# Gated attention's first three norm sums taken as two rounded products each

## The reference, cut to what matters

```
def rms_norm_2(x, gain):
    x32 = x.astype(jnp.float32)
    y = x32 * lax.rsqrt(jnp.mean(x32 * x32, axis=-1, keepdims=True) + EPS)
    return (y * gain.astype(jnp.float32)).astype(x.dtype)
```

## Time and profile before

| what | us |
|---|---|
| median of 3 runs | 2284.31 |
| lowest and highest run | 2283.43, 2285.08 |
| the profiled execution, its own time | 2283.69 |
| its span, first to last instruction | 2281.9 |
| TensorE busy | 2270.4 |
| VectorE busy | 1677.5 |
| ScalarE busy | 1321.6 |

### The profile page before, as it was taken

The page is one execution under the profiler, slowest core; times in us unless marked ns, Lnnn a source line. Parts: engine busy times, 40 slices in busy tenths (PEclk is TensorE's granted clock), DMA queues, the critical chain, the costliest instruction groups (busy, mean ns, idle before and its releaser), DMA issues.

```text
span 2281.9 us, 36209 instructions
## 1 busy us (share of the span) xinstructions
PE 2270.4 (99%) x14199; PEld 1997.4 (88%) x14199; DVE 1677.5 (74%) x2130; ACT 1321.6 (58%) x1630; POOL 66.3 (3%) x104
## 2 busy tenths in 40 slices
PE   8999999999999999999999999999999999999999
PEld 7888888988888889889888888998888888889888
DVE  7876678787667666778776776688875677777773
ACT  7554567566456445675654654666654565467552
POOL 3200002000000000000000000000000000000000
PEclk9999999999999999999999999999999999999999
DMA  8655656565555555545655555534555565644653
GB/s 252 205 186 192 189 159 167 174 202 184 186 186 190 193 184 181 158 149 184 199 189 191 187 188 184 173 107 151 185 184 188 181 195 191 212 130 153 191 190 129
DMA packets 344946, 411.91 MB, mean 181 GB/s; under 512 B 7812, under 2 KB 291926, under 8 KB 344704
## 3 DMA queue, kind: packets, MB, share of 16 engines
q1 hardware_dynamic: 340432, 399.30, 54.0%
q0 software_dynamic: 4176, 10.95, 2.0%
q10 hardware_dynamic: 224, 0.07, 0.0%
HBM read 409.08 MB, written 1.21 MB: 180 GB/s over the span
## 4 chain that ended last, share of the span: by engine, by line
PE 97%; DVE 1%; DMA 1%; ACT 0%; issue 0%; SPq 0%; DVEq 0%; ACTq 0%
PE ps L605 54%; PE ps L608 27%; PE ps L633 2%; PE ps L634 1%; PE ps L635 1%; PE ps L650 1%; PE ps L652 1%; PE ps L651 1%; PE ps L902 1%; PE ps L979 1%; PE ps L980 1%; PE ps L981 1%; PE ps L931 1%; PE ps L915 1%; DMA raw<-in_w_mem_kv 0%; PE ps L1113 0%
## 5 line engine op out<-in xcount | busy, mean ns | idle before, releaser
L605 PE MATMUL ps<-h,whi 128*128 128x512 f32 x3552 | 1120.7, 396 | 0.1
L1983 DVE TENSOR_TENSOR wlo<-raw,whi 128x2048 fp32r<-128x2048 f32 x375 | 859.0, 2292 | 272.1 <-ACT whi L1340 270.9
L1340 ACT ACTIVATE whi<-raw 128x2048 fp32r<-128x2048 f32 x376 | 719.6, 1915 | 268.4 <-DMA raw<-in_ffn_w_down 157.2
L608 PEld LDWEIGHTS ps<-h,wlo 128*128 128x128 f32 x3552 | 666.3, 188 | 161.8
L608 PE MATMUL ps<-h,wlo 128*128 128x256 f32 x3552 | 702.6, 279 | 0.0
L605 PEld LDWEIGHTS ps<-h,whi 128*128 128x128 f32 x3552 | 539.1, 188 | 6.4 <-issue 5.7
L605 PE MATMUL ps<-act,whi 128*128 128x512 f32 x1408 | 444.7, 396 | 0.0
L1383 ACT ACTIVATE accT<-ps 128x512 f32<-128x512 f32 x227 | 135.4, 596 | 372.8 <-PE ps L608 372.2
L608 PEld LDWEIGHTS ps<-act,wlo 128*128 128x128 f32 x1408 | 264.7, 188 | 65.8
L608 PE MATMUL ps<-act,wlo 128*128 128x256 f32 x1408 | 278.4, 278 | 0.0
L1992 DVE TENSOR_TENSOR accT<-ps,accT 128x512 f32<-128x512 f32 x200 | 138.2, 691 | 166.3 <-ACT accT L1383 165.0
(11 more groups left out here) (407 smaller groups left out, 2329.2 us busy)
## 6 DMA issues: line engine op xcount, KB each, us to landing
raw<-in_ffn_w_gate SPq DMA_DIRECT2D x88, 1024.0 KB, 5.3
raw<-in_ffn_w_up SPq DMA_DIRECT2D x88, 1024.0 KB, 5.3
raw<-in_ffn_w_down SPq DMA_DIRECT2D x88, 1024.0 KB, 5.0
raw<-in_w_in SPq DMA_DIRECT2D x30, 1024.0 KB, 5.4
raw<-in_w_gate SPq DMA_DIRECT2D x24, 1024.0 KB, 5.4
raw<-in_w_in_a SPq DMA_DIRECT2D x13, 1024.0 KB, 5.2
raw<-in_w_branch SPq DMA_DIRECT2D x12, 1024.0 KB, 5.1
raw<-in_w_o SPq DMA_DIRECT2D x8, 1024.0 KB, 5.2
```

The lines of the kernel that those rows point to most:

```text
L605: mm(dst, whi[:, r, col:col + P], rhs, start=first, stop=False, skip_group_check=True)
L608: return mm(dst[:, 0:SEQ], wlo[:, r, col:col + P], rhs[:, 0:SEQ], start=False, stop=last, skip_group_check=True)
L1340: fn(whi[:, gr % RING, :], raw[:, gr % RING, :], ACT.Copy).then_inc(hi_done, 1)
L1983: v.tensor_tensor(wlo[:, gr % RING, :], raw[:, gr % RING, :], whi[:, gr % RING, :].bitcast(F32), ALU.subtract)\
```

## The change

The sums of the first three pairs in the stage `fox` become two products of rounded (fp32r) operands each, added in PSUM; the fourth pair's sum stays as it is.

- ScalarE's squares are written in the rounded format (`qn_r` or `sq_r[:, 6:8]`, the same memory as before). They are the high part, and no instruction is added on ScalarE.
- VectorE squares the same pair again in full float32 into a free part of `sq` (`tensor_tensor`, 128x512), waits for ScalarE's square, and subtracts the high part in place (`low_part`, 128x512), which leaves the low part. Both stand right behind the scaling of slots 0, 1 and 2, and `low_part` signals the new semaphore `qn_low`.
- TensorE waits for `qn_low` in place of `qn_sq` and runs `two_parts`: `blk_r` times the high part, `blk_r` times the low part, in the same place of the order as the product at L731.
- `blk_r`, a rounded copy of `blk` (128x128), is made once by VectorE in slot 0 of the stage `kv`, some 230 us earlier.
- `sq` gets a second view of type fp32r at the same place, and its allocation grows by 32 bytes, so that what lies behind it moves by that much.

The diff, cut to its core:

```diff
+            def two_parts(b, high, low):
+                fill(b)
+                mm(ps[:, b, :], blk_r[:, :], high, start=True, stop=False)
+                mm(ps[:, b, :], blk_r[:, :], low, start=False, stop=True).then_inc(filled[b], 1)
+
-            def qk_norm(src=qn, b=7):
+            def qk_norm(src=qn, b=7, low=None):
                 n.q += 1
+                if low is not None:
+                    n.low += 1
+                    pe.wait_ge(qn_low, n.low)
+                    two_parts(b, src[:, :, :].rearrange("p a n -> p (a n)"), low.rearrange("p a n -> p (a n)"))
+                    return
                 pe.wait_ge(qn_sq, n.q)
...
                             if s_ == 2:
                                 pe.wait_ge(summed, n.e + 2)
-                                qk_norm(qn, 3)
+                                qk_norm(qn_r, 3, low=sq_r[:, 2:4, :])
                             elif s_ in (3, 4):
-                                qk_norm(qn if s_ == 3 else sq[:, 6:8, :], 3)
+                                qk_norm(qn_r if s_ == 3 else sq[:, 6:8, :], 3, low=sq_r[:, 2:4, :] if s_ == 3 else None)
...
-                            hooks = {2: third, 3: lambda: qk_norm(sq[:, 6:8, :])}
+                            hooks = {2: third, 3: lambda: qk_norm(sq_r[:, 6:8, :], low=sq_r[:, 4:6, :])}
...
-                            qk_squares(fqm[:, :, :], (summed, n.e + 1), free=1)
+                            qk_squares(fqm[:, :, :], (summed, n.e + 1), qn_r, 1)
...
-                            qk_squares(fq[:, 0:2, :], (summed, n.e + 2), sq[:, 6:8, :], 1)
+                            qk_squares(fq[:, 0:2, :], (summed, n.e + 2), sq_r[:, 6:8, :], 1)
...
-                            qk_squares(fq[:, 2:4, :], (summed, n.e + 3), free=1)
+                            qk_squares(fq[:, 2:4, :], (summed, n.e + 3), qn_r, 1)
...
+            def low_part(low, full, high, squares):
+                dve.wait_ge(qn_sq, squares)
+                v.tensor_tensor(low, full, high.bitcast(F32), ALU.subtract).then_inc(qn_low, 1)
...
+                        if s == 0:
+                            v.tensor_copy(blk_r[:, :], blk)
...
                         v.tensor_tensor(dst, src, rstd2, ALU.mult).then_inc(summed, 1)
+                        if s < 3:
+                            k, high = (4, sq_r[:, 6:8, :]) if s == 1 else (2, qn_r[:, :, :])
+                            full = sq[:, k:k + 2, :]
+                            dve.wait_ge(summed, n.e + s + 1)
+                            link(v.tensor_tensor(full, dst, dst, ALU.mult))
+                            low_part(sq_r[:, k:k + 2, :], full, high, q0 + s + 1)
```

More of the change, by code:

```diff
@@ L92, in __init__ @@
         self.q = 0
+        self.low = 0
         self.post = 0
@@ L236, in mixed_transformer @@
         xT = sb("xT", [P, KT, SEQ])
-        sq = sb("sq", [P, KT, SEQ])
+        sq_base = (nc.sbuf_base + 31) // 32 * 32
+        sb("squares", [P, KT * SEQ + 8])
+        sq = nc.alloc_sbuf_tensor_at("sq", [P, KT, SEQ], F32, offset=sq_base)
+        sq_r = nc.alloc_sbuf_tensor_at("sq_r", [P, KT, SEQ], F32R, offset=sq_base)
         h = sb("h", [P, KT, 2 * SEQ], F32R)
@@ L259, in mixed_transformer @@
         qn = nc.alloc_sbuf_tensor_at("qn", [P, 2, SEQ], F32, offset=qn_base)
+        qn_r = nc.alloc_sbuf_tensor_at("qn_r", [P, 2, SEQ], F32R, offset=qn_base)
         hll = nc.alloc_sbuf_tensor_at("hll", [P, 2, TT, P], F32R, offset=qn_base)
@@ L283, in mixed_transformer @@
         junk = at("junk", 68 * K, [P, D_MODEL])
+        qm_r = at("qm_r", 64 * K, [P, DEPTH, 2, SEQ], F32R)
+        junk_r = at("junk_r", 68 * K, [P, D_MODEL], F32R)
         diag = at("diag", 72 * K, [P, 4, P])
@@ L289, in mixed_transformer @@
         onat = at("onat", 0, [P, TT, D_MODEL])
+        blk_r = at("blk_r", 87 * K + 512, [P, P], F32R)
         act = at("act", 0, [P, FT, 2 * SEQ], F32R)
@@ L368, in mixed_transformer @@
         qn_sq, qn_rs, qn_done = sem("qn_sq"), sem("qn_rs"), sem("qn_done")
+        qn_low, mk_low = sem("qn_low"), sem("mk_low")
         f_gate, lf_done = sem("f_gate"), sem("lf_done")
@@ L1408, in qk_norm, with qk_squares @@
                 qk_roots()
-            def qk_squares(src, ready, dst=qn, free=0):
+            def qk_squares(src, ready, dst=qn, free=0, full=None):
                 act_e.wait_ge(*ready)
@@ L1413, in qk_squares @@
                     act_e.wait_ge(qn_done, n.q - free)
+                if full is not None:
+                    fn(full, src, ACT.Square)
                 fn(dst[:, :, :], src, ACT.Square).then_inc(qn_sq, 1)
@@ L2806, in step @@
                         scaled(i)
+                    q0 = n.q
                     for s in range(7):
```

## The result

The changed kernel takes 2287.22 us (20 runs, 2286.85 to 2287.98) against 2283.77 us for the kernel before (20 runs, 2283.01 to 2285.08): a ratio of 1.0015, 95% interval 1.001 to 1.0021. It is 3.45 us slower where 1.2 us faster was forecast.

The account below looks back on a forecast made before the run. The prediction took TensorE, busy in 99% of the span, as the bound. Three sums saving 1.17 us, all else at nothing, took the profiled 2283.69 to 2282.5 us and the median from 2284.31 to 2283.1, range 2281.4 to 2285.1.

Parts of the forecast that it names:

- last sign of being wrong: Whole span: the prediction is wrong if what the stage `fox` gains is not in the span.
- The bound: Whole kernel: TensorE, busy in 99% of the span, sets the time; what it is spared in `fox` reaches the end.
- The sums: Stage `fox`, TensorE: two rounded products replace one float32 product of 0.86 us, saving 0.39 us a sum, 1.17 for three.
- The row of the mix stage: Mix stage's two-part sum, same shape: 0.23 us each, taken as the price of a rounded product 128x512.
- the rival in which a float32 product takes twice a rounded one: Sums in `fox`: both kinds of sum cost the same, no gain, about 2284.3 us; no-gain chance 0.10.
- VectorE: Behind the first three scalings in `fox`: additions of 1.46 us a pair, 4.4 for three, taken at nothing as covered.
- the margins: Time VectorE's additions have to spare in `fox`: 0.94 us at the second sum, 0.4 to 0.8 at unit 0's transposes.
- The copy of the blocks: Stage `kv`, VectorE: one rounded copy 128x128, taken at nothing, bound 0.2 us.
- the rest: Memory behind `sq` moving 32 bytes and seven more VectorE instructions: taken at nothing, 0.5 us either way.
- The slower rivals: Sums and VectorE in `fox`: float32 price for the new products, chance 0.03, or additions too late, chance 0.02.
- the first of them: Three sums in slots 2 and 3: `blk_r` products at float32 price, 2.6 us lost, about 2286.9 us; chance 0.03.

Follow-up runs that it names:

- e2: Changed kernel with the allocation behind `sq` kept at its old size, so nothing moves: 2282.42 us against 2283.74 for the kernel before, ratio 0.9996.
- e8: Changed kernel without the 32-byte shift, VectorE making each full square three times: 2284.75 us against 2283.60 for the kernel before, ratio 1.0006.
- e1: Kernel before with only 32 unused bytes added behind `sq`, moving `h` and the arena: 2288.62 us against 2283.74, ratio 1.0021.
- e6: Kernel before with `whi` alone 32 bytes lower, `wlo`, `h` and the arena staying: 2263.55 us against 2283.60, ratio 0.9912.
- e5: Kernel before with 32 unused bytes in front of the weight ring, so weights, `h` and arena move together: 2283.50 us against 2283.60, ratio 0.9999.
- e12: Changed kernel without the shift, `whi` 32 bytes lower, `h` at 98528 and the arena at 137184: 2297.80 us, ratio 1.0061 to the kernel before.
- e7: Kernel before with 128 unused bytes behind `sq`, putting `h` at 98592 and the arena at 137280: 2285.55 us, ratio 1.0009.

## Why the prediction was wrong

The measured 2287.22 us lie 2.1 us above the range of 2281.4 to 2285.1. The prediction's last sign of being wrong came true: what the stage gained is not in the span, which grew by 3.5 us.

The bound was read rightly: TensorE sets the time, and what changes on it reaches the end. That held for the loss as well as for the gain.

The sums: 0.39 us each were forecast, 1.17 together. e2 has 1.18 in the trace and 1.32 in the medians. The row of the mix stage was the right price, 0.23 us, and the float32 product was worth nearly four of them; the rival in which a float32 product takes twice a rounded one, and the saving is nil, fell with it: 0.86 us against 0.23. The Trainium skill ("Perfetto Trace Analysis", section "Engine Utilization") has the array's output rate halved for FP32_LOW_HIGH products; if that is the format of this sum, the trace has it at little over a quarter. The 215.7 ns that the Trainium skill ("TensorE: Matmul & The Clock Gate", section "Wait — 56ns, not 53.3ns?") has for a product of 512 columns doesn't hold here: a group would be 2 x 215.7 + 2 x 109.2 = 650 ns by it, an estimate from that page, which names no type of operand for the figure, and the best groups of any run took 690.

VectorE: 1.46 us a pair, measured 1.46; no wait of TensorE in the stage; the reduction behind the third pair starts 0.17 us after it. e8 shows that the margins were real and, to 0.2 us, of the size that was worked out.

The copy of the blocks: 0.22 us, nothing behind it.

The step that failed is the last one, "the rest". It said that the memory behind `sq` moves by 32 bytes, that no row prices it, and took nothing, with 0.5 us either way. It measured 4.88 us (e1), ten times that bound, and it stands against hundreds of groups of products all over the kernel, not against three sums. Where no row shows a resource the cost should have been bounded by what uses it: 2480 groups of four products at 700 ns are 1736 us, so each per cent of a product's step is 17 us. A range of 0.5 us meant a claim that a shift changes a product by less than a thirtieth of a per cent, and nothing in the trace said so. The trace of before did hold a hint, though not in the means, 699.9 and 700.1 ns: the same four instructions at other addresses gave other single steps, with `act` 668 of 695 at 700 ns, with `h` 1092 of 1726 at 696 to 698 and 545 at 705 to 706. When the shift put `h` where `act` had been, relative to the weights, 1609 of its steps became 700 as well. So the place already showed in the trace before, though not what a shift would cost.

The slower rivals named two mechanisms, float32 prices for the new products and a late VectorE; neither happened. That the first of them had 2286.9 us, near the measured 2287.22, is luck: it had the three sums at 0.86 us a product, and they took 0.23.

What stays open is what collides. The time depends on how the streamed operand lies relative to both weight buffers, and on how these lie to each other. Products with `whi` and with `wlo` alternate, and each loads its weights while the one before it streams, so two reads of on-chip memory run side by side. In the kernel before, the weights from `wlo` are loaded beside the wide product that starts at 1206.48 us and the narrow one behind it:

```profile
1206.48 0.42 PEld L608 LDWEIGHTS ps<-act,wlo 128*128 128x128 f32 x2
```

A rival is that reads or writes by others get in TensorE's way, since ScalarE, VectorE and the DMAs use the same buffers. The traces speak against it. The steps with `act` during which ScalarE and VectorE both rest for over nine tenths of the step average 700.0 ns in the kernel before and 705.5 in the changed one (67 and 68 steps); those during which both work average 699.9 and 706.3 (55 and 57). With no DMA packet under way the steps average 699.9 and 706.1 (134 and 136). With all of them at rest together there are only 12 and 14 steps, and they average 700.0 and 706.6. And the cycle of 704 and 709 ns goes on unchanged through whole phases of 61 us, while the others start and stop. So the loss is there when nobody else works, and what is left to meet are TensorE's own accesses. Which of them, no run shows. It isn't just the stream and the load that run at the same moment: during the first wide product of a group only `whi` is loaded, yet with the streamed operand 32 above `whi` that product's step was 235.7 ns with `act` in the kernel before, where it lies 64 above `wlo`, and 227.0 with `h` in e6, where it lies 32 above `wlo`.

The Trainium skill ("TensorE: Matmul & The Clock Gate", section "Step-by-step: what each phase is for") says that loading the next weights takes no read bandwidth from the running product, since TensorE has two read ports. No run here separates the load from the stream, so none decides that; what the runs add is that the step of the same products is not independent of where the weights lie, since moving `whi` alone by 32 bytes changed it by 1.4%.

## What to carry to other kernels

Where one engine is busy for 99% of the span, look at every allocation that a change touches before its instructions: 32 bytes of padding outweighed the whole change here. Compare addresses before and after, keep them equal when an instruction-level change is to be judged, and try a few shifts of the large operands as an optimisation of its own; it gave 20 times what the change gave. To find such a loss, compare the length of equal phases in the two traces; if phases far from the edit grew, it isn't the edit's instructions. Take that length from the starts in order of time, not from the busy sums of the profile's page.

## What the runs showed of the hardware

- A wide product of rounded operands costs more or less by the relative place of its operands in on-chip memory: 690 to 708 ns for a group of 2 x 512 and 2 x 256 columns, at a granted clock of 1.000 throughout. The slow place costs as much when ScalarE, VectorE and the DMAs all rest: 706.6 against 700.0 ns (after, before).
- A float32 product of 128x512 holds TensorE for 0.86 us (before), one of two rounded operands for 0.23 us (after, e2).
- Moving all operands by the same 32 bytes changes nothing (e5, ratio 0.9999).
- The best places seen have `whi` and `wlo` alike modulo 128 and the streamed operand 64 above both (690 ns), the worst ones the streamed operand 96 above `whi` or above `wlo` (705 to 708 ns).
- The steps of such groups repeat in a fixed cycle of one to four, which differs by place: 700 ns each (`act` before), 704 and 709 in turn (`act` after). One place has two cycles, of 706.7 and 700.0 ns (e12).
- The mean of groups of four repeats at 128 bytes (e7). That of narrow products with `h`, of 256 columns, doesn't: 353.4 against 358.6 ns for three.
